# VectorE's weight sums, convolution sides and modulation products order themselves by semaphores instead of drains; eight modulation loads move earlier, and VectorE takes over one multiplication from GpSimd

## The reference, cut to what matters

```python
def first_block(x, ...):                     # D_MODEL 2048, SEQ 256, D_FF 5632
    h = rmsnorm(x, norm_mix)
    proj = h @ w_in                          # stages "proj" and "gate"
    ...window attention A, neighbourhood attention B...
    merged = (sigmoid(ga) * (out_a @ w_branch_a)      # stage "branch"
              + sigmoid(gb) * (out_b @ w_branch_b))
    x = x + merged @ w_out                   # stage "wout"
    u = rmsnorm(x, norm_ffn) @ w_up          # stage "up"
    up = jnp.pad(u, ((0, 0), (1, 1), (0, 0)))
    u = up[:, :-2] * cw[0] + up[:, 1:-1] * cw[1] + up[:, 2:] * cw[2] + conv_b
    gate, val = jnp.split(u, 2, axis=-1)
    return x + (silu(gate) * val) @ w_down   # stage "down"

def trunk_layer(x, xc, c_act, cc_act, w_mod, b_mod, ...):
    mod_x = split(c_act @ w_mod + b_mod, 6)  # w_mod is 2048 x 12288
    mod_c = split(cc_act @ w_mod + b_mod, 6)
    ...linear attention over ctx and x, spatial gating...   # "ctx", "mix", "wout2"
    f_x = swiglu(modulate(rms_norm(x, g_pre_ffn), mod_x[3], mod_x[4]), w_ffn_in, w_ffn_out)
    return x + mod_x[5] * rms_norm(f_x, g_post_ffn)         # "up2", "down2"
```

## Time and profile before

| | before |
|---|---|
| median of 3 runs | 2772.25 us (2771.92 to 2775.7) |
| the profiled execution | 2773.26 us |
| its span, first to last instruction | 2771.5 us |
| TensorE busy | 2741.2 us |
| VectorE busy | 2153.1 us |
| ScalarE, GpSimd busy | 583.7 us, 336.8 us |

### The profile page before, as it was taken

How to read it: one execution, slowest core, us unless ns; L and a number is a source line. 1 busy time by engine, 2 the same in 40 slices (tenths; PEclk the granted TensorE clock), 3 DMA queues, 4 the chain that set the end, 5 groups by cost and what they waited for, 6 DMA issues and landing times.

```text
span 2771.5 us, 30348 instructions
## 1 busy us (share of the span) xinstructions
PE 2741.2 (99%) x10948; PEld 1937.3 (70%) x10948; DVE 2153.1 (78%) x3128; ACT 583.7 (21%) x1219; POOL 336.8 (12%) x462
## 2 busy tenths in 40 slices
PE   9999999999999999999999999999999999999998
PEld 8888888886444444468888888888544444448887
DVE  7888788988999999998887568976776767555554
ACT  3221112001353443530002121211221111211000
POOL 1011221000112212120111002200001010000000
PEclk9999999999999999999999999999999999999999
DMA  8787666677766666668886455555567676565553
GB/s 277 244 255 220 207 207 205 213 244 228 222 209 217 215 208 217 205 204 288 281 290 197 140 164 139 160 160 175 166 221 220 212 221 204 176 174 188 175 175 122
DMA packets 276358, 571.45 MB, mean 206 GB/s; under 512 B 25370, under 2 KB 26778, under 8 KB 275696
## 3 DMA queue, kind: packets, MB, share of 16 engines
q1 hardware_dynamic: 244528, 460.18, 53.7%
q0 software_dynamic: 31248, 109.01, 12.1%
q10 hardware_dynamic: 432, 0.34, 0.0%
HBM read 565.49 MB, written 3.93 MB: 205 GB/s over the span
## 4 chain that ended last, share of the span: by engine, by line
PE 65%; issue 16%; DVE 11%; DVEq 6%; ACT 1%; POOLq 0%; POOL 0%; DMA 0%; ACTq 0%
PE PS L597 44%; PE PS L612 15%; DVEq L1141 4%; DVE sums L1144 3%; DVE mem L1493 2%; DVE ring L1130 2%; DVE sums L1146 1%; DVE sums L1129 1%; DVE mem L1266 1%; ACT mem L2093 1%; PE PS L659 1%; DVEq L1175 1%; PE PS L783 0%; PE PS L752 0%; DVE mem L1178 0%
## 5 line engine op out<-in xcount | busy, mean ns | idle before, releaser
L597 PE MATMUL PS<-ring,mem 128*128 128x256 f32 x3088 | 863.4, 380 | 4.5 <-DVE mem L1172 3.8
L597 PE MATMUL PS<-sums,mem 128*128 128x256 f32 x2656 | 790.0, 379 | 0.0
L597 PEld LDWEIGHTS PS<-ring,mem 128*128 128x128 f32 x3088 | 582.5, 190 | 85.7 <-DVE mem L1172 4.6
L597 PEld LDWEIGHTS PS<-sums,mem 128*128 128x128 f32 x2656 | 504.6, 190 | 68.6
L612 PE MATMUL PS<-ring,act_t 128*128 128x512 f32 x1056 | 512.8, 593 | 9.8 <-DVE mem L1172 8.6
L612 PEld LDWEIGHTS PS<-ring,act_t 128*128 128x128 f32 x1056 | 199.2, 190 | 260.1 <-issue 241.5
L612 PE MATMUL PS<-sums,mem 128*128 128x512 f32 x704 | 359.5, 592 | 0.0
L1132 DVE TENSOR_TENSOR sums<-ring 128x512 f32<-128x512 f32 x255 | 177.5, 696 | 221.0 <-PE PS L597 199.8
L1266 DVE SCALAR_TENSOR_TENSOR mem<-mem,small 128x1024 f32<-128x1024 f32 x240 | 305.1, 1292 | 36.5 <-DMA mem<-in_w_mod 20.1
L1915 ACT COPY first_q<-PS 128x256 f32<-128x256 f32 (+1 forms) x76 | 33.0, 434 | 1158.6 <-PE PS L597 692.4
L2415 POOL DMA_DIRECT2D mem<-in_w_mod x192 | 104.0, 542 | 1357.8 <-DVE mem L1266 1151.6
(11 more groups left out here) (289 smaller groups left out, 2149.0 us busy)
## 6 DMA issues: line engine op xcount, KB each, us to landing
ring<-in_w_in SPq DMA_DIRECT2D x240, 512.0 KB, 3.8
mem<-in_w_mod POOLq DMA_DIRECT2D x192, 512.0 KB, 4.7
ring<-in_w_up SPq DMA_DIRECT2D x176, 512.0 KB, 4.4
ring<-in_w_ffn_in SPq DMA_DIRECT2D x176, 512.0 KB, 4.5
ring<-in_w_down SPq DMA_DIRECT2D x88, 512.0 KB, 4.3
ring<-in_w_ffn_out SPq DMA_DIRECT2D x88, 512.0 KB, 3.6
ring<-in_w_out SPq DMA_DIRECT2D x64, 512.0 KB, 3.7
ring<-in_w_branch_a SPq DMA_DIRECT2D x16, 512.0 KB, 3.7
```

The source lines that it names most:

```text
L597: mm = pe.matmul(product(g, j), of(j, 2 * (c if part is None else part) + q), weights(j, n, q), start=lead and j in OPENS, stop=tail, skip ...
```

## The change

1. `step_last` has no drains. The first, third and fourth operations raise `sums_ready`; the third waits for the first's count and the fourth for the third's. TensorE waits for 3n+3 instead of n+1.
2. `conv_sides` has no drain; each of its 8 operations raises `up_convolved`, and the second pass waits for the first pass's operation on the same row.
3. `mod_halves` waits for `wm_used` of the half before instead of draining.
4. `HALVES`: four more halves in `gate` (the last chunk of every second group), four more in `branch`, eight fewer in `down` (single instead of double). GpSimd's counts of loads follow. The total stays 192.
5. The product of the two halves in the first feed-forward is made by VectorE behind the value sides (j = 4). It waits for Silu (`up_g_act`) and for its own last side. GpSimd waits for `hidden_done`, and its drain between that and the combinations is gone.
6. In the second feed-forward SP stores the gate row (`store_gate(1)`) behind the third chunk of `down2` instead of ahead of the first, and loads it back behind the ninth instead of the fourth.

```diff
 for _k in range(8):
-    for _j in range(1, 4 if _k % 2 else 3):
+    for _j in range(1, 4):
         HALVES[N0["gate"] + 4 * _k + _j] = 1
-for _k in range(1, 16, 2):
-    HALVES[N0["branch"] + _k] = 1
+for _k in range(16):
+    if _k % 4 != 2:
+        HALVES[N0["branch"] + _k] = 1
...
-    HALVES[N0["down"] + _k] = 2 if _k in (21, 22, 28, 29, 30, 31, 32, 39, 40, 41) else 1
+    HALVES[N0["down"] + _k] = 2 if _k in (24, 30) else 1
...
-                if n_up == N0["up2"]:
-                    store_gate(1)
...
-                        if n_up == N0["up2"] and (g, c) == (0, 3):
+                        if n_up == N0["up2"] and (g, c) == (0, 2):
+                            store_gate(1)
+                        if n_up == N0["up2"] and (g, c) == (0, 8):
                             load_gate(1, gate_bc2)
...
-                pe.wait_ge(s["sums_ready"], n + 1)
+                pe.wait_ge(s["sums_ready"], 3 * n + 3)
...
             def step_last(m):
...
-                ve.tensor_tensor(to[:, 1], to[:, 0], b22, ADD)
-                ve.drain()
-                ve.tensor_tensor(to[:, 2], to[:, 1], b21, ADD).then_inc(s["sums_ready"], 1)
+                _, _, b21, b22, one, two, three = blocks_of(n)
+                ve.wait_ge(s["sums_ready"], 3 * n + 1)
+                ve.tensor_tensor(two, one, b22, ADD).then_inc(s["sums_ready"], 1)
+                ve.wait_ge(s["sums_ready"], 3 * n + 2)
+                ve.tensor_tensor(three, two, b21, ADD).then_inc(s["sums_ready"], 1)
...
-                    ve.drain()
+                    if h:
+                        ve.wait_ge(s["wm_used"], h)
                     ve.wait_ge(wm_loaded[h % 2], 16 * (h // 2 + 1))
...
-                    if side == 0:
-                        ve.drain()
-                op.then_inc(s["up_convolved"], 1)
+                            ve.wait_ge(s["up_convolved"], before + f + 1)
+                        ve.scalar_tensor_tensor(o, beside_, conv[:, k, 2 * side:2 * side + 1], o, MUL, ADD)\
+                            .then_inc(s["up_convolved"], 1)
...
                 if j == VALUE_SIDES:
                     conv_sides(up_v4, conv_v, i, "up_v_based", KF)
+                    h4 = hidden[:, 4 * i:4 * i + 4, :]
+                    ve.wait_ge(s["up_g_act"], i + 1)
+                    ve.wait_ge(s["up_convolved"], 16 * i + 16)
+                    ve.tensor_tensor(h4, h4, up_v4, MUL).then_inc(s["hidden_done"], 1)
...
-                        if i:
-                            ve.wait_ge(s["up_g_act"], i)
-                            ve.wait_ge(s["hidden_done"], i)
...
-                    pool.wait_ge(s["up_g_act"], i)
-                    pool.wait_ge(s["up_convolved"], 2 * i)
-                    pool.tensor_tensor(h4, h4, up_v4, MUL).then_inc(s["hidden_done"], 1)
+                    pool.wait_ge(s["hidden_done"], i)
                     mod_loads(1)
-                    pool.drain()
                     combine(*pairs_of(i - 1), "forms_h")
```

More of the change, by code:

```diff
@@ L1115, in step, with blocks_of @@
                 step_last(m)
+            def blocks_of(n):
+                if n in WIDE_CHUNKS:
+                    return (*wide_weights(n), *(wide_sum(n, k) for k in range(3)))
+                w, to = ring[:, n % SLOTS], sums[:, n % TSLOTS]
+                return (w[:, :, 0, 0:256], w[:, :, 0, 256:512], w[:, :, 1, 0:256], w[:, :, 1, 256:512],
+                        to[:, 0], to[:, 1], to[:, 2])
             def step_first(m):
@@ L1196, in combine_pair, with first_sums @@
                 ve.tensor_tensor(e[:, 2], q[:, 1, 0], e[:, 1], ADD).then_inc(s[done], 1)
-            def first_sums(q, done):
+            def first_sums(q, done, count):
                 w, to = ring[:, 0, q], sums[:, 0, :, q]
@@ L1206, in first_sums @@
                 ve.drain()
-                ve.tensor_tensor(to[:, 2], to[:, 1], b21, ADD).then_inc(s[done], 1)
+                ve.tensor_tensor(to[:, 2], to[:, 1], b21, ADD).then_inc(s[done], count)
             def combine_q(q, e, done):
@@ L1483, in conv_sides @@
             def conv_sides(dst, src, i, based, at_):
+                before = 16 * i + (8 if at_ else 0)
                 ve.wait_ge(s[based], i + 1)
@@ L2495, in _ @@
             norm_rstd("ctx")
-            mod_loads(28)
+            mod_loads(20)
             pool.wait_ge(s["wm_used"], 160)
```

47 lines of the change are left out of this document (13 added, 34 removed).

## The result

The changed kernel takes **2757.39 us** (median of 4 runs, 2757.24 to 2757.78), against 2773.65 us for the kernel before in the same session (4 runs, 2771.92 to 2775.7). The ratio is 0.9942, with a 95% interval of 0.9927 to 0.9957. The forecast was 2757.0.

The account below looks back on a forecast made before the run. TensorE is busy nearly throughout, and VectorE's lateness costs it 15.9 us; less 0.5 us kept, 15.4 us off 2773.26 gives 2757.9, and 1.0 less for the median gives 2757.0 us. Range: 2754.5 to 2763.

Parts of the forecast that it names:

- The accounting: TensorE's 11 stops behind VectorE: 13.0 us drawn plus 0.26 us each, 15.9 us in all, of which 15.4 go.
- Steps: In each step the third sum starts 0.60 us behind the second, saving 0.16 us; the fourth, 0.73 to 0.77, saves nothing.
- rival A: The flush can't be avoided: removing drains saves nothing, only moving the product gives 0.77 us a group; 2761 us, chance 0.08.
- Rival C: VectorE waiting for its own semaphore is dearer than the drain: some 2790 us, chance 0.05; milder form, within 0.2%, 0.05.
- Halves and sides: In modulation halves and side passes each removed drain saves 0.16 us: 0.64 and 0.32 us a group of `up`.
- The product: In `up`, moving it to VectorE nets 0.77 us a group; combinations' stretch unchanged; 3 us of cover for Silu.
- The reserve: In `up` VectorE gets 3.0 us a group back, enough to cover every stop, and 1.7 us a group stay over.
- One sign: In `up` VectorE should again wait for TensorE in most steps.
- What was left: Blocks of doubled halves end in groups 4 and 8 of `up`; 0.25 us each stays there (0 to 0.9).
- The store: The 0.7 us stop ending `up2` goes; the load of `down2`'s fourth chunk is late, 9.4 us of cover for 8.7.
- What moved earlier: Extra halves in `gate` (2.4 us of cover), `branch` (+0.6 us) and `wout` (+4.6 us) cost TensorE nothing.
- rival B: `wout` or `gate` fall behind and TensorE waits there: 4.6 us back, 2761.6 us, chance 0.06.

Follow-up runs that it names:

- idle reductions: The kernel after with two unused VectorE reductions of 128x1024 added in every group of `up`: 2763.74 us.
- three reductions: The kernel after with three unused VectorE reductions of 128x1024 added in every group of `up`: 2774.99 us.

## Why the prediction came out right, point by point

**The accounting.** 11 stops at 13.0 + 11 x 0.26 = 15.9 us, of which 15.4 should go: from profiled execution to profiled execution 2773.26 - 2757.78 = 15.5 went. The view of waits confirms that all 11 are gone, so by the same accounting 15.9 should have gone. The starts of the same matmul record in both traces show where the 0.4 us is. Ahead of 100 us the kernel after is 0.36 us later than the kernel before, and from there to the end it gains 15.85 us. So the estimate of 0.26 us a stop was right, and the 0.5 us that the prediction kept back for groups 4 and 8 happened to meet 0.4 us at the start.

**Steps.** The third sum is 0.60 us behind the second, as taken. The fourth is 0.72, at the low end of 0.73 to 0.77: a step saves 0.16 + 0.05 = 0.21 us, not 0.16. Alone it gave 8.8 us. The section of the Trainium skill that the prediction set against this ("VectorE: DVE Perf Modes", "The DRAIN you can't avoid") says that the flush can't be skipped by leaving out semaphores, and also, in a sentence that the prediction passed over, that a next operation which isn't held starts earlier. The trace agrees with the second: the starts are 0.60 us apart for operations of 0.68. So rival A had less behind it than the prediction wrote. Rival C is out: the engine's own semaphore cost 0.05 us less than the drain where one operation needs the last.

**Halves and sides.** 0.16 us each, confirmed by rows: the sides take 3.24 for 3.40, and a half starts 0.61 us behind a sum instead of 0.78. On their own they carry 0.5 us of the time.

**The product: the step that failed.** The prediction said "I move that cost and don't change it" of the combinations' stretch. It also read only two of three stretched sums, 0.90 us of 1.27. The stretch grew from 1.27 to 1.56 us a group with the product alone and to 1.7 in the kernel after. So on the kernel before the product brought not 0.77 but 0.77 - 0.29 = 0.5 us a group by the stretch, 0.4 by the stops without the lower clock, and 0.2 by the medians (2.4 us in 11 groups). The forecast survived, because the group had 1.7 us in reserve by its own sum. The other part of the step held: Silu was 4.4 us ahead, against "3 us of cover".

**The reserve.** 3.0 us saved less 1.3 a group gave 1.7; the chip has about 3.0 in ordinary groups and 0.6 in those with a block's end. The average of 1.3 mixed long stops with short ones; the steps gave 0.4 us a group more than counted; and the stretch gives way. One sign fails by it: VectorE was to wait for TensorE "in most steps", and does so in three of eight in an ordinary group and in none of the groups 5 and 9.

**What was left.** 0.25 us each was forecast at the ends of groups 4 and 8, and nothing is there. VectorE is indeed latest there: its first sum of the next group starts 3.6 us after TensorE began that group (905.22 and 901.60), and 2.3 us after it in an ordinary one (951.93 and 949.66). The end of group 4, both engines:

```profile
900.68 1.21 DVE L1168 TENSOR_TENSOR mem<-PS,first_q 128x1024 f32<-128x1024 f32 x1
...
901.60 1.88 PE L613 MATMUL PS<-ring,act_t 128*128 128x512 f32 x4
```

The gather's first operation is done at 901.89. Q1 is the first two of these four records, and the third, which needs the gather, starts at 902.46: 0.6 us of cover, the reserve that the idle reductions found. Behind group 5 it is 948.60 against 950.52, 1.9 us. So no stop follows, but the margin is small.

**The store.** Predicted: the fourth chunk's load of `down2` late by 8.7 us with 9.4 of cover. Measured: 6.7 us and no stop. Undone, it costs 1.1 us at the place named.

**What moved earlier.** `gate` and `wout` have no stop, as forecast. In `branch` the sum was +0.6 us "where VectorE has 11.1 us idle in 100". That was the wrong way to read it. What mattered was one hand-over at its end, with 0.5 us of cover, which no step of the prediction looked at. The merge came 0.6 us earlier instead, 0.9 as TensorE sees it, since the kernel after is 0.36 us later from its start on. The fourth sum's 0.05 us in 16 steps are 0.8 us of this difference of 1.5; the rest isn't accounted for. With the drains in place the same table costs a stop of 2.1 to 2.5 us there. This is rival B's "idle time in an average can lie in the wrong place", but at the end of `branch` and not in `wout`.

**Rival A's price.** It was given as 2761 and, with its condition made, came out at 2774.84. Three terms were wrong at once: the product's 0.77; the end of `branch` and the start of `up`, where the saved drains had to pay for the table (4.0 us); and the stops' own size, since they don't shrink in proportion. The table alone doesn't explain it: with the drains and without the table, the product alone took 2770.71 us, still 10 us over rival A's price, of which moving the store would have given some 1 to 2. Rivals A and B were treated as apart, and A brings B with it. The range, whose high end was "A and B", would have been missed by 12 us in that case.

## What to carry to other kernels

A saving on an engine that is late by little counts in full only until the other engine stops waiting; after that it is reserve. The drains of halves and sides cost 0.5 us on the kernel after, and 16.0 us where the steps' drains are back too. So price a rival with all its consequences, not with one term, and look for the hand-over with the least cover rather than for idle time in an average. When work moves from one engine to another, look at what then runs beside what: holding GpSimd's combinations back until VectorE gathers from PSUM gave 10 us for one wait.

## What the runs showed of the hardware

- Two VectorE operations of 0.69 us (128x512 float32) start 0.60 us apart with nothing between them or with a wait that is long met, 0.72 apart where the second waits by semaphore for the first, and 0.76 to 0.78 apart with a drain.
- A GpSimd addition of 128x256 takes 0.72 us beside a gather from PSUM and up to 1.2 us beside VectorE's sums in SBUF, which in turn take up to 1.2 instead of 0.69.
- Behind some long stops TensorE's granted clock fell to its lower level (1.2 GHz). It did so for about 7 us behind a stop drawn with 2.99 us and for about 3.4 us behind one of 2.98 (three reductions), behind the first of two of 2.02 (all drains back) and behind one of 2.30 (product alone). It stayed at 1.00 behind the second one of 2.02 in the same execution, and in the kernel before behind stops of 2.29 and 3.07 us. What makes the difference stays open.
